# Where ten layers meet: slabs by token tile at each end, token-major openings, and a reordered end of the mixer

## Chip, cores and metric

The kernel runs on one core of one Trainium2 chip. The metric is the device time of one execution in microseconds (us). Beside the runs there is one profiled execution, from which every row below comes.

## What is computed

The reference is a two-block hybrid transformer on 256 tokens of width D = 1024, in float32. Cut to its layers, each with what follows it:

```python
x = LN(a*x + 0.5*swiglu(x))            # phase 0, FFN, 2816 hidden
x = LN(a*x + hybrid_mixer(x))          # phase 1, MIXER
x = LN(a*x + 0.5*swiglu(x))            # phase 2, FFN          a = 2**0.25
h = h + 0.5*swiglu(rms(h))             # phase 3, FFN
h = h + short_conv(rms(h))             # phase 4, CONV: (b * conv(c*u)) @ w_out, b, c, u = split(rms(h) @ w_in)
h = h + 0.5*swiglu(rms(h))             # phase 5, FFN
shared = shared_kv(rms(h))             # phase 6, KV: keys, values, and compressed ones by a GELU MLP
h = h + 0.5*swiglu(rms(h))             # phase 7, FFN
h = h + nsa(rms(h), *shared)           # phase 8, NSA: compressed, selected and window attention, gated
h = h + 0.5*swiglu(rms(h))             # phase 9, FFN
```

The mixer is three attentions of six heads each (MOBA, DIFF, STICK). Each is projected by its branch matrix and weighted by a sigmoid gate, and the sum goes through w_out.

## The kernel before

**Slabs.** All large weights go through one ring of six slots. A slab is 128 x 2048 values (1 MB): half of a 512-wide column block of a projection (kh = 0 or 1, four chunks of 128 rows), or two rows of 128 x 1024 of a matrix that ends a layer. SyncE loads slab k with two DMAs when slab k - 6 has been used (semaphore slab_used). ScalarE (ACT) writes its high half w_hi, VectorE (DVE) the rest w_lo = raw - w_hi. TensorE (PE) makes each product from three matmuls: low by high, high by low, high by high (function product, L1562 to L1564). The input of a layer, transposed, is split in the same way into xT_hi (ACT, L632) and xT_lo (DVE, L977).

**Order.** Each engine has an instruction list written out by hand; there is no planner. On ACT and DVE the call split(k) stands between the other work, LEAD = 4 slabs ahead of the one in use. The semaphores high_ready and low_ready carry them to the next engine. Phases 0 to 9 take 33, 36, 33, 33, 16, 33, 10, 33, 8 and 33 slabs. Tokens are two tiles of 128 (tt = 0, 1).

**End of a layer.** project_slab adds up a closing projection in four PSUM banks Y[tt][half]. All but the last two slabs are taken with both token tiles. Of the last two, first all products of tile 0 are made, which signals y_ready, and then all of tile 1. Meanwhile DVE handles tile 0 in boundary: add_output (L992), layer_norm (L999 to L1002), a root by GpSimd (POOL, L567), layer_norm_apply (L1010, L1012), and rms_norm (L1017, L1023) for which ACT sums the squares (L643). Behind the last product, next_input transposes tile 0 for the next layer (L1571). GpSimd multiplies x by ALPHA beforehand (L606).

**Beginning of a layer.** by_token lets the first column block (two slabs) run over tile 0, puts in the transposes of tile 1, and then runs over tile 1. FFN, MIXER and NSA begin so. CONV and KV begin with slabs by feature, which need the whole input (feature_slab).

**Mixer.** TILES is the order of the column blocks, STEPS how many slabs TensorE takes before head u. Round u + 1 of slabs stands between heads u - 1 and u. DVE forms the maxima (L1141, L1149) and the weights (L1171 to L1180) of a head, normalizes the pairs of DIFF heads (L1188 to L1203), and multiplies branches by gates (L1122 to L1126). The last round is gate 1, branch 0 and branch 1 of STICK, then z_sb is transposed and w_out begins.

**Shared keys.** Slabs 0 and 1 give the raw tokens of the compression by feature. ACT and DVE spread them into xc_hi (L826) and xc_lo (L1317). Slabs 2 and 3 are slot 0 of keys and values, 4 to 7 the compression, 8 and 9 slot 1. ACT applies the GELU (L850) once DVE has made its bias (L1352) from the transposed hidden rows.

**NSA.** Slabs 0 and 1 give the queries of eight heads, then 48 products give the branch gates, then slabs 2 and 3 give the other queries. DVE sums the squares of the queries (L1386), GpSimd takes the roots (L596), DVE scales (L1396) and copies the transposed queries (L1405).

## Time and profile before

| | us |
|---|---|
| median of 3 runs | 1751.81 |
| lowest and highest | 1748.11 and 1752.46 |
| profiled execution, its own time | 1752.8 |
| its span, first to last instruction | 1751.1 |
| TensorE busy (8310 matmuls) | 1677.5 |
| VectorE, ScalarE, GpSimd busy | 968.9, 743.0, 44.3 |

The mean granted clock of TensorE over the span is 0.975 of 2.4 GHz. In the windows below, PE, DVE, ACT and POOL are the engines' busy time; PEld is the weight load, which overlaps PE. Matmuls are pipelined: one of 512 columns is shown with nearly 0.4 us and the next starts 0.23 behind it, so a wait shows as idle only beyond that overlap.

### The profile page before, as it was taken

How to read it: one execution, taken by the hardware profiler on the slowest of the kernel's cores; microseconds unless marked ns; L12 is line 12 of the kernel's file. 1: busy time of each engine (PE TensorE's matmuls, PEld its weight loads, DVE VectorE, ACT ScalarE, POOL GpSimd, SP SyncE). 2: the span in 40 equal slices, each digit the busy share in tenths (PEclk: the TensorE clock that was granted, in tenths of full speed). 3: DMA queues.
4: the chain of work that ended last, by engine and by line, in shares of the span. 5: the costliest groups of instructions: out<-in, count | busy, mean ns of one | idle time of the engine just before them, and what ended most of it. 6: DMA issues, size and time to landing. Idle time of an engine off the chain costs nothing.

```text
span 1751.1 us, 19663 instructions
## 1 busy us (share of the span) xinstructions
PE 1677.5 (96%) x8310; PEld 1402.8 (80%) x8310; DVE 968.9 (55%) x1016; ACT 743.0 (42%) x907; POOL 44.3 (3%) x56
## 2 busy tenths in 40 slices
PE   7999999898799998999999999989999998999998
PEld 6888797776678886888799888878888887888887
DVE  5555557575565546555357555557655454555552
ACT  4544244555344433444234444436444334544441
POOL 1000100000010000000000000000000010000000
PEclk9999999999899999999989999999999997999999
DMA  8565654433455654565546565457465541045551
GB/s 266 178 207 192 193 186 139 133 96 110 136 172 178 222 192 136 182 199 192 180 133 204 170 191 200 175 159 233 153 189 205 175 155 48 1 140 183 184 190 73
DMA packets 226088, 291.13 MB, mean 166 GB/s; under 512 B 10516, under 2 KB 203728, under 8 KB 225872
## 3 DMA queue, kind: packets, MB, share of 16 engines
q1 hardware_dynamic: 226000, 289.87, 50.3%
q8 instruction: 66, 1.08, 0.3%
q14 instruction: 22, 0.18, 0.0%
HBM read 288.78 MB, written 1.05 MB: 166 GB/s over the span
## 4 chain that ended last, share of the span: by engine, by line
PE 88%; DVE 7%; ACT 2%; issue 2%; DMA 0%; POOL 0%; SPq 0%; DVEq 0%; ACTq 0%
PE bank L1562 27%; PE bank L1564 27%; PE bank L1563 26%; DVE w_lo L971 2%; PE bank L1675 2%; PE bank L1961 1%; PE bank L1986 1%; PE bank L1571 1%; PE bank L1971 1%; ACT w_hi L626 1%; DVE xT_lo L977 1%; DVE x_sb L992 1%; ACT xT_hi L632 0%; DMA raw<-in_ffn_w_up_dram 0%; PE bank L2001 0%
## 5 line engine op out<-in xcount | busy, mean ns | idle before, releaser
L971 DVE TENSOR_TENSOR w_lo<-raw,w_hi 128x2048 fp32r<-128x2048 f32 x268 | 609.6, 2286 | 324.9 <-ACT w_hi L626 323.4
L626 ACT ACTIVATE w_hi<-raw 128x2048 fp32r<-128x2048 f32 x268 | 505.0, 1900 | 153.1 <-DMA raw<-in_ffn_w_down_dram 101.0
L1562 PE MATMUL bank<-w_hi,xT_lo 128*128 128x512 f32 (+1 forms) x1328 | 531.3, 400 | 30.1 <-DVE xT_lo L977 17.3
L1564 PE MATMUL bank<-w_hi,xT_hi 128*128 128x512 f32 (+1 forms) x1328 | 521.5, 393 | 0.0
L1563 PE MATMUL bank<-w_lo,xT_hi 128*128 128x512 f32 (+1 forms) x1328 | 520.9, 392 | 0.0
L1562 PEld LDWEIGHTS bank<-w_hi,xT_lo 128*128 128x128 f32 x1328 | 253.7, 191 | 84.5 <-DVE xT_lo L977 20.1
L1564 PEld LDWEIGHTS bank<-w_hi,xT_hi 128*128 128x128 f32 x1328 | 253.2, 191 | 53.5
L1563 PEld LDWEIGHTS bank<-w_lo,xT_hi 128*128 128x128 f32 x1328 | 253.7, 191 | 49.1
L1562 PE MATMUL bank<-w_hi,hT_lo 128*128 128x512 f32 x528 | 209.1, 396 | 0.0
L1563 PE MATMUL bank<-w_lo,hT_hi 128*128 128x512 f32 x528 | 208.6, 395 | 0.0
L1564 PE MATMUL bank<-w_hi,hT_hi 128*128 128x512 f32 x528 | 208.6, 395 | 0.0
L923 ACT ACTIVATE hT_hi<-bank 128x512 fp32r<-128x512 f32 x66 | 39.5, 598 | 213.3 <-PE bank L1675 213.3
L935 ACT ACTIVATE silu<-bank 128x256 f32<-128x256 f32 x132 | 43.6, 381 | 193.4 <-PE bank L1564 193.4
L1564 PEld LDWEIGHTS bank<-w_hi,hT_hi 128*128 128x128 f32 x528 | 99.3, 188 | 23.7
L1563 PEld LDWEIGHTS bank<-w_lo,hT_hi 128*128 128x128 f32 x528 | 99.4, 188 | 23.4
L1562 PEld LDWEIGHTS bank<-w_hi,hT_lo 128*128 128x128 f32 x528 | 99.3, 188 | 23.4
L1562 PE MATMUL bank<-xT_hi,w_lo 128*128 128x256 f32 x368 | 108.4, 295 | 6.8 <-DVE w_lo L971 4.0
L1563 PE MATMUL bank<-xT_lo,w_hi 128*128 128x256 f32 x368 | 107.5, 292 | 0.0
L1564 PE MATMUL bank<-xT_hi,w_hi 128*128 128x256 f32 x368 | 107.4, 292 | 0.0
L1512 DVE TENSOR_TENSOR hT_lo<-bank,hT_hi 128x512 fp32r<-128x512 f32 x66 | 45.6, 691 | 99.6 <-ACT hT_hi L923 99.5
L1523 DVE TENSOR_TENSOR h<-silu,bank 128x256 f32<-128x256 f32 x132 | 49.6, 417 | 74.9 <-ACT silu L935 74.9
L1562 PEld LDWEIGHTS bank<-xT_hi,w_lo 128*128 128x128 f32 x368 | 74.1, 201 | 8.8 <-issue 5.0
(246 smaller groups left out, 1241.0 us busy)
## 6 DMA issues: line engine op xcount, KB each, us to landing
raw<-in_ffn_w_gate_up_dram SPq DMA_DIRECT2D x176, 512.0 KB, 4.7
raw<-in_ffn_w_down_dram SPq DMA_DIRECT2D x132, 512.0 KB, 4.0
raw<-in_ffn_w_gate_dram SPq DMA_DIRECT2D x44, 512.0 KB, 3.9
raw<-in_ffn_w_up_dram SPq DMA_DIRECT2D x44, 512.0 KB, 5.0
raw<-in_w_in_dram SPq DMA_DIRECT2D x44, 512.0 KB, 4.9
raw<-in_conv_w_in_dram SPq DMA_DIRECT2D x24, 512.0 KB, 4.5
raw<-in_kv_w_dram SPq DMA_DIRECT2D x12, 512.0 KB, 4.4
raw<-in_w_out_dram SPq DMA_DIRECT2D x8, 512.0 KB, 3.6
```

Source lines behind the costliest of these rows:

```text
L626: nc.scalar.activation(w_hi[:, slot, 0:width], raw[:, slot, 0:width], ACT.Copy).then_inc(high_ready, 1)
L923: nc.scalar.activation(hT_hi[:, 2 * j:2 * j + 2, :], bank[4 + j % 2][:].rearrange("p (c m) -> p c m", c=2), ACT.Copy).then_inc(hT_high, 1)
L935: nc.scalar.activation(silu[:, tt, :], bank[2 * (j % 2) + tt][:, 0:256], ACT.Silu).then_inc(silu_ready, 1)
L971: nc.vector.tensor_tensor(w_lo[:, slot, 0:width], raw[:, slot, 0:width], w_hi[:, slot, 0:width].bitcast(F32), ALU.subtract).then_inc(low_r ...
L977: nc.vector.tensor_tensor(xT_lo[:, 4 * q:4 * q + 4, tt * P:(tt + 1) * P], src[:].rearrange("p (k m) -> p k m", k=4), xT_hi[:, 4 * q:4 * q ...
L992: ins = nc.vector.scalar_tensor_tensor(out=part, in0=Y[tt][half][:], scalar=factor, in1=part, op0=ALU.mult, op1=ALU.add)
L1512: nc.vector.tensor_tensor(hT_lo[:, 2 * j:2 * j + 2, :], bank[4 + j % 2][:].rearrange("p (c m) -> p c m", c=2), hT_hi[:, 2 * j:2 * j + 2, : ...
L1523: nc.vector.tensor_tensor(h[:, tt, :], silu[:, tt, :], bank[2 * (j % 2) + tt][:, 256:512], ALU.mult).then_inc(h_ready, 1)
L1562: nc.tensor.matmul(o, x_lo, wh, start=first, stop=False, skip_group_check=shared)
L1563: nc.tensor.matmul(o, x_hi, wl, start=False, stop=False, skip_group_check=shared)
L1564: return nc.tensor.matmul(o, x_hi, wh, start=False, stop=last_one, skip_group_check=shared)
L1675: ins = nc.tensor.transpose(dst[:, c, tt * P:(tt + 1) * P], h[:, tt, c * P:(c + 1) * P], ident[:])
```

## The change

Layers end with tail(n) slabs by token tile: four where LN and RMS follow, else three. Tile 0's transposes for the next layer stand ahead of the last slab of tile 1. Each layer but the first begins with four slabs by token. CONV opens with its b gate by token, copies it (conv_b) and transposes it in sixteen transposes; KV opens with slots 0 and 1, the raw tokens come third, and tile 1 of slot 1 behind them. The compressed products move into the next FFN. In NSA all queries precede the gates. In the mixer the order of blocks and steps changes, splits run MIX_LEAD = 5 ahead, and its end takes gate 1 around branch 0. Splits are counted (split_to) instead of placed one by one. The factor ALPHA goes into add_output, with x and the epsilon scaled to match.

```diff
+TAIL = 3
+MIX_LEAD = 5
+        def tail(n):
+            return TAIL + 1 if has_ln(n) and has_rms(n) else TAIL
-        TILES = [("v of moba, sb",), ("q, k of moba",), ("k of moba, q of diff",), ("q, k of diff",), ("v of diff",),
-                 ("gate", MOBA, 0), ("gate", MOBA, 1), ("branch", MOBA, 0), ("branch", MOBA, 1),
-                 ("q, k of sb",), ("k, v of sb",), ("gate", DIFF, 0), ("gate", DIFF, 1), ("branch", DIFF, 0), ("branch", DIFF, 1),
+        TILES = [("v of moba, sb",), ("v of diff",), ("q, k of moba",), ("k of moba, q of diff",), ("q, k of diff",),
+                 ("gate", MOBA, 0), ("gate", MOBA, 1), ("q, k of sb",), ("branch", MOBA, 0), ("branch", MOBA, 1),
+                 ("k, v of sb",), ("gate", DIFF, 0), ("gate", DIFF, 1), ("branch", DIFF, 0), ("branch", DIFF, 1),
                  ("gate", STICK, 0), ("gate", STICK, 1), ("branch", STICK, 0), ("branch", STICK, 1)]
+        MIX_SLABS += [(16, 0), (17, 0), (16, 1), (18, 0)]
-        STEPS = [6] + [1] * 8 + [2] * 3 + [1] * 4 + [2, 1, 1] + [4]
+        STEPS = [8] + [1] * 8 + [2] + [1] * 6 + [2, 1, 1] + [4]
...
 # ACT
+            def split_to(k):
+                while highs[0] <= k:
+                    split(highs[0])
+                    highs[0] += 1
             def boundary(n):
+                split_to(first_slab[n + 1] + 5 - tail(n))
+                if n < last:
                     for tt in range(NT):
                         norm(n, [tt])
                         evacuate_input(inputs_before(n + 1), TOKENS_FIRST[2 * tt:2 * tt + 2], 2 * tt)
+                        if tt == 0:
+                            split_to(first_slab[n + 1] + 3)
...
 # ACT, mixer's end
+                    gate_half(STICK, 0)
+                    split_to(s0 + 34)
+                    evacuate_input(inputs_before(n) + 1, MERGED_FIRST[0:2])
+                    gate_half(STICK, 1)
+                    split_to(s0 + 35)
+                    evacuate_input(inputs_before(n) + 1, MERGED_FIRST[2:4], 2)
...
 # ACT, KV
+                    for kv in range(2):
+                        split_to(s0 + 10 + 2 * kv)
+                        act.wait_ge(slab_used, s0 + 8 + 2 * kv)
                         nc.scalar.activation(hid_row[:, kv, :], bank[6 + kv][0:CMP_ROWS, 0:CMP_HID], ACT.Copy).then_inc(hid_rows, 1)
+                        if kv == 1:
+                            evacuate_input(inputs_before(n + 1), TOKENS_FIRST[0:2])
                         act.wait_ge(bias_ready, kv + 1)
...
 # DVE
             def boundary(n, factor, y_at):
+                split_to(first_slab[n + 1] + 5 - tail(n))
                 for tt in range(NT):
                     add_output(n, tt, factor, y_at)
                     if has_ln(n):
+                        layer_norm(n, tt, factor)
+                        if tt == 1:
+                            split_to(first_slab[n + 1] + (2 if has_rms(n) else 3))
+                        layer_norm_apply(n, tt)
+                    if tt == 1:
+                        split_to(first_slab[n + 1] + 3)
+                    if has_rms(n):
+                        rms_norm(n, tt)
+                    if n < last:
+                        evacuate_input(inputs_before(n + 1), TOKENS_FIRST[2 * tt:2 * tt + 2], 2 * tt)
...
 # DVE, KV
+                    keys_spread(1)
+                    keys_norm(1)
+                    split_to(s0 + 9)
                     for tt in range(NT):
                         rms_norm(n, tt)
                     for kv in range(2):
-                        split(s0 + 8 + 2 * kv)
-                        split(s0 + 9 + 2 * kv)
+                        split_to(s0 + 10 + 2 * kv)
+                        if kv == 1:
+                            evacuate_input(inputs_before(n + 1), TOKENS_FIRST[0:2])
                         dve.wait_ge(hidT_psum, kv + 1)
...
 # DVE, NSA
                     queries_norm(0)
-                    split(s0 + 5)
-                    split(s0 + 6)
-                    queries_out(0)
+                    split_to(s0 + 5)
                     queries_spread(1)
                     queries_norm(1)
+                    split_to(s0 + 6)
+                    queries_out(0)
...
 # PE, in place of project_slab
+                for tt in range(NT):
+                    for d in range(first, slabs):
+                        if tt == 0:
+                            ready(d)
+                            pe.wait_ge(low_ready, s0 + d + 1)
+                        elif d == slabs - 1 and n < last:
+                            next_input(n + 1, 0)
+                        for c in range(2):
+                            ins = part(d, c, tt)
+                        if tt == 1:
+                            ins.then_inc(slab_used, 1)
+                        elif d == slabs - 1:
+                            ins.then_inc(y_ready, 1)
...
+            def by_token(n, works, second=3):
                 for tt in range(NT):
+                    for i, work in enumerate(works):
+                        if tt == 0 and i == second:
                             next_input(n, 1)
+                        pe.wait_ge(xT_ready, 4 * inputs_before(n) + 2 * tt + min(i, 1) + 1)
+                        work(tt)
...
 # PE, mixer's end
+                    for d in ROUND[-1][:-1]:
                         slab(d)
                     pe.wait_ge(merged, 10)
+                    transpose_input(z_sb, MERGED_FIRST[0:2])
+                    slab(ROUND[-1][-1])
...
 # PE, KV
+                    by_token(n, [pairs(slot, kh) for slot in range(2) for kh in range(2)], 2)
                     for kh in range(2):
+                        ins = feature_slab(s0 + 4 + kh, kh, [bank[4], bank[5]], 4)
+                    ins.then_inc(cmp_in_psum, 1)
+                    keys_values(1, 0, 1).then_inc(slab_used, 1)
+                    keys_values(1, 1, 1).then_inc(slab_used, 3)
```

In by_token, second is 2 where the layer before ends without LN.

## Rows read from the trace of the kernel before

**Rows 1.** The page's part 1: busy us of each engine (share) xinstructions.

```profile
PE 1677.5 (96%) x8310; PEld 1402.8 (80%) x8310; DVE 968.9 (55%) x1016; ACT 743.0 (42%) x907; POOL 44.3 (3%) x56
```

**Rows 2.** Waits of TensorE: us in total, times, longest.

```profile
PE bank L1562 <- DVE xT_lo L977: 20.2, 13, 7.6
PE bank L1562 <- DVE w_lo L971: 14.0, 3, 6.0
```

**Rows 3.** Windows: length, busy us (x), PEclk, DMA share, GB/s.

```profile
320.00:340.00 20.00, 16.01 (x113) 15.20 (x111) 11.23 (x22) 8.12 (x18) 0.00 (x0) 0.83 0.33 106
...
440.00:464.00 24.00, 14.47 (x62) 11.41 (x60) 13.23 (x13) 6.60 (x6) 0.00 (x0) 0.79 0.29 92
478.00:494.00 16.00, 13.07 (x57) 10.19 (x56) 10.62 (x15) 3.68 (x5) 3.23 (x3) 0.89 0.42 132
664.00:692.00 28.00, 21.42 (x88) 16.95 (x87) 16.22 (x24) 6.03 (x9) 3.21 (x4) 0.88 0.34 112
868.00:888.00 20.00, 14.68 (x75) 13.18 (x74) 13.25 (x15) 9.86 (x11) 1.10 (x2) 0.74 0.33 106
...
1160.00:1180.00 20.00, 14.64 (x84) 13.14 (x84) 13.55 (x20) 10.06 (x12) 1.10 (x2) 0.83 0.45 138
1220.00:1232.00 12.00, 11.02 (x67) 9.20 (x66) 9.39 (x24) 6.94 (x14) 2.15 (x2) 1.00 0.36 117
...
1430.00:1444.00 14.00, 14.00 (x69) 12.34 (x69) 9.50 (x9) 6.88 (x7) 3.26 (x2) 0.76 0.34 139
```

**Rows 4.** Timeline of DVE at two boundaries: start, us, instruction [idle].

```profile
668.30 1.29 DVE L992 SCALAR_TENSOR_TENSOR x_sb<-bank,x_sb 128x512 f32<-128x512 f32 x2 [7.12 <-PE bank L1564]
...
673.34 1.28 DVE L1012 SCALAR_TENSOR_TENSOR x_sb<-x_sb,stats,gain 128x1024 f32<-128x1024 f32 x1
...
677.56 1.28 DVE L1023 SCALAR_TENSOR_TENSOR z_sb<-x_sb,stats,gain 128x1024 f32<-128x1024 f32 x1
...
866.79 1.29 DVE L992 SCALAR_TENSOR_TENSOR x_sb<-bank,x_sb 128x512 f32<-128x512 f32 x2 [7.27 <-PE bank L1564]
...
870.11 1.29 DVE L1023 SCALAR_TENSOR_TENSOR z_sb<-x_sb,stats,gain 128x1024 f32<-128x1024 f32 x1 [0.66 <-POOL stats L567]
872.39 1.29 DVE L992 SCALAR_TENSOR_TENSOR x_sb<-bank,x_sb 128x512 f32<-128x512 f32 x2 [0.99 <-PE bank L1564]
```

**Rows 5.** The page's parts 5 and 6: splits and loads of slabs.

```profile
L971 DVE TENSOR_TENSOR w_lo<-raw,w_hi 128x2048 fp32r<-128x2048 f32 x268 | 609.6, 2286 | 324.9 <-ACT w_hi L626 323.4
L626 ACT ACTIVATE w_hi<-raw 128x2048 fp32r<-128x2048 f32 x268 | 505.0, 1900 | 153.1 <-DMA raw<-in_ffn_w_down_dram 101.0
...
raw<-in_ffn_w_gate_up_dram SPq DMA_DIRECT2D x176, 512.0 KB, 4.7
```

**Rows 6.** Timeline of DVE in the rounds of DIFF.

```profile
326.87 1.02 DVE L1141 SCALAR_TENSOR_TENSOR prob<-far,bank 128x384 f32<-128x384 f32 x2 [0.71 <-PE bank L1776]
...
333.20 2.29 DVE L971 TENSOR_TENSOR w_lo<-raw,w_hi 128x2048 fp32r<-128x2048 f32 x1
...
338.08 0.43 DVE L1203 TENSOR_TENSOR oT_lo<-o_norm,oT_hi 128x256 fp32r<-128x256 f32 x1 [0.48 <-ACT oT_hi L732]
```

**Rows 7.** Timeline of ACT and of DVE at the shared keys.

```profile
1185.86 4.91 ACT L826 ACTIVATE xc_hi<-bank 64x512 fp32r<-64x512 f32 x8 [6.15 <-PE bank L1564]
...
1212.69 0.52 ACT L850 ACTIVATE hid<-bank,cmp_bias 128x64 f32<-128x64 f32 x2 [5.58 <-DVE cmp_bias L1352]
...
1188.34 5.72 DVE L1317 TENSOR_TENSOR xc_lo<-bank,xc_hi 64x512 fp32r<-64x512 f32 x8 [3.94 <-ACT xc_hi L826]
...
1201.14 0.76 DVE L1335 TENSOR_TENSOR key_n<-bank,key_ms 128x256 f32<-128x256 f32 x2 [1.76 <-POOL key_ms L600]
...
1206.83 1.28 DVE L1023 SCALAR_TENSOR_TENSOR z_sb<-x_sb,stats,gain 128x1024 f32<-128x1024 f32 x1 [0.66 <-POOL stats L567]
```

**Rows 8.** Timeline of POOL and of DVE at the queries of NSA.

```profile
1451.95 3.24 POOL L596 TENSOR_TENSOR q_ms<-q_ms,minus_half 128x8 f32<-128x8 f32 x2 [14.17 <-DVE q_ms L1387]
...
1449.13 1.41 DVE L1405 TENSOR_SCALAR qT<-bank,cols 128x512 f32<-128x512 f32 x2 [6.16 <-PE bank L1925]
```

More of the change, by code:

```diff
@@ L47 @@
 PHASES = [FFN, MIXER, FFN, FFN, CONV, FFN, KV, FFN, NSA, FFN]
-BY_TOKEN = (FFN, MIXER, NSA)
+CONV_AT = PHASES.index(CONV)
 LENGTH = {FFN: 33, MIXER: 36, CONV: 16, KV: 10, NSA: 8}
@@ L811, in _ @@
-                    for d in range(KC // 2 - 2):
-                        split(s0 + 12 + d + LEAD)
+                    split_to(s0 + 4)
+                    for half in range(2):
+                        act.wait_ge(slab_used, s0 + 2 * half + 2)
+                        for tt in range(NT):
+                            nc.scalar.activation(conv_b[:, tt, 512 * half:512 * (half + 1)], bank[2 * half + tt][:], ACT.Copy)\
+                                .then_inc(conv_b_ready, 1)
+                        split_to(s0 + 5 + 2 * half)
@@ L1209, in tiles @@
                                 tile_out(ends(d))
-                    def slabs(steps):
-                        for d in steps:
-                            split(s0 + d + LEAD)
                     for d in ROUND[0]:
@@ L1250, in _ @@
+                    tile_out(TILES.index(("branch", STICK, 0)))
+                    split_to(s0 + 34)
+                    tile_out(TILES.index(("gate", STICK, 1)))
+                    evacuate_input(inputs_before(n) + 1, MERGED_FIRST[0:2])
+                    tile_out(TILES.index(("branch", STICK, 1)))
+                    split_to(s0 + 35)
+                    evacuate_input(inputs_before(n) + 1, MERGED_FIRST[2:4], 2)
                     boundary(n, 1.0, s0 + 36)
-                    for d in range(KC // 2 - 2, KC // 2):
-                        split(s0 + 32 + d + LEAD)
@@ L1681, in tile, with first_tiles, work @@
                         gate_up(j, 1)
-                    by_token(n, lambda kh, tt: gate_up(0, kh, tiles=[tt]))
+                    def first_tiles(j, kh):
+                        def work(tt):
+                            if behind_kv(n) and (j, kh, tt) == (1, 0, 0):
+                                pe.wait_ge(key_normed, 2)
+                            gate_up(j, kh, [tt])
+                            if behind_kv(n) and (j, kh, tt) == (0, 0, 0):
+                                transpose_hidden(1)
+                            if behind_kv(n) and (j, kh, tt) == (0, 0, 1):
+                                compressed()
+                            if (j, kh, tt) == (1, 0, 1):
+                                hidden(0)
+                        return work
+                    if n == 0:
+                        by_token(n, [first_tiles(0, kh) for kh in range(2)])
+                        tile(1)
+                    else:
+                        by_token(n, [first_tiles(j, kh) for j in range(2) for kh in range(2)], 2 if not has_ln(n - 1) else 3)
                     def transpose_keys(slot, b):
```

537 lines of the change are left out of this document (232 added, 305 removed).

## The prediction, made before the change was run

> **What bounds the kernel now.** I read the page first: TensorE is busy 1677.5 us of a span of 1751.1, so it sets the time, and only what leaves it idle or slow can be won [rows 1]. The waits of TensorE say whom it waits for: for the low halves of the layer's input, 20.2 us in 13 waits, the longest 7.6; for low halves of weights, 14.0 us in three, of which 6.0 is the first load, so that two are 4.0 [rows 2]. The windows then show where, and what each stretch loses beside the idle time: the reader is to see PE busy below the length, and PEclk below 1.00 in the same stretch [rows 3]. PEclk 0.83 over 20 us means 6.8 us at 1.2 instead of 2.4 GHz; what TensorE does in them takes twice as long. So the mixer's first wait costs 4.0 idle and some 3.1 of slow clock; there are two of them. The mixer's end loses 9.5 idle and 2.3 clock; the boundary FFN to FFN 6.6 and 3.1; FFN to convolution 5.3 and 3.2; FFN to shared keys 5.4 and 2.5. Boundaries without LN where the next layer already opens by token lose 1.0 to 1.1 and no clock (1220:1232; those at 974, 1415 and 1557 are alike).
>
> The other engines are loose in the mean (DVE 55%), but they run in order, and what matters below is what stands ahead of the needed instruction. Unit costs: twelve products of one token tile and one slab take 2.8 us (the two adds of one boundary start 5.60 apart, with 24 products between) [rows 4]. A slab that comes free is split 9.4 us later: landing 4.7, high half 1.9, low half 2.3, and 0.5 for issuing [rows 5]. From the first add to the normalized tile DVE needs 6.3 us with LN, 10.5 with LN and RMS, 4.6 with RMS alone [rows 4]; without the two operations for the other tile that stand inside the 10.5, it is 9.7.
>
> **Projections end with three or four slabs by token, layers open with four (all nine boundaries).** Call T the start of the last three slabs. The first token tile is ready at T+8.4 (before: two slabs, 5.6), the second takes as long, and the transposes for the next layer now stand before its last slab, so 5.6 us of products cover the norm and the last 2.8 cover the 2.6 that ACT and DVE need to split the transposed tile. The price is a slab less of lead: before the first add DVE must split the next layer's third slab, whose slot is free only at T, so the add starts at T+9.4.
> - RMS alone (five: 872, 974, 1165, 1415, 1557 us): normalized at T+14.0, TensorE there at T+14.0: no wait. Second tile: add 1.3, a split 2.3, spread, root and scaling 2.1 make 5.7 against two slabs of the new layer, 5.6: 0.2 wait. At the convolution this leaves 0.3 of 5.3 and no slow clock: -8.2 with the 3.2; with the second tile's transposes now under products, another 1.0: -9.2. At the shared keys 5.4+2.5 go the same way: -7.9. The three that lost 1.1 give 0.8 each: -2.4, of which NSA's is counted below, so -1.6.
> - LN alone, FFN to mixer: normalized at T+9.4+6.3=T+15.7, 1.7 late; second tile 0.4 and 0.5, because a slab of v of diff is narrower. Before, 2.8 in three waits. 0.
> - LN alone, mixer to FFN: the three waits of 1.0 and half of 3.4 us of clock (478:494) [rows 3] become one wait of 1.9: -2.7.
> - LN and RMS, FFN to FFN, four slabs: no late split (11.2 before the first add). The tile comes 9.7 after the add, cover is 8.4: 1.3. Second tile: add and statistics 3.0, split 2.3, LN 2.6, split 2.3, RMS 2.1 = 12.3 against three slabs, 8.2: a wait of 4.1 where before it was 1.0, and slow clock again, 2.5. 5.4+2.5 for 6.6+3.1: -1.8.
> - The scaling of x by ALPHA on GpSimd goes into the add's scalar, an operation of the same form; it ran beside splits for which TensorE did not wait: 0. Were that cover gone, three splits a little slower would be at stake, some 3 us in all.
>
> **Mixer.** v of diff moves to the front, q, k of sb two rounds earlier, splits run five slabs ahead instead of four. The two low halves that were late are then split three rounds sooner. Their 8.0 idle and 6.2 clock go. But the three double rounds of DIFF become one. DVE needs 6.3 us from a head's scores to its weights with a split in it (326.87 to 333.20) and in every second round 3.1 more for the pair's norm (to 338.51), plus 0.7 for the copy of v of sb [rows 6]; TensorE has 5.8 of a slab, 0.9 of outputs and 0.3 of transposes for it. So 10.1 stand against 6.8: one wait of 3.2 at the twelfth head, 0.5 in small ones, and 2.5 of clock: 14.2 become 6.2, -8.0. The bounds are none of it (-12, the splits being earlier still) and a wait in every second of the rounds. At the end, the gate's second half is computed between the branches, so that transposes, sigmoids and half of the sums lie under 4.1 us of branch and 5.6 of first projection slab. DVE has nothing left behind the last branch but 2.7 for 5.6 of products. All of the idle time there goes, 9.5, and 2.3 of clock: -11.8. A wait would take its place only if banks 6 and 7, into which the first transposes now go, were read late; attention has left them a slab before.
>
> **Convolution.** Four slabs of 5.8 become token slabs of 5.5 (-1.2), 16 transposes of 0.11 are added (+1.8): +0.6. DVE has 10.6 us of work for each 11.5 of products.
>
> **Shared keys.** Time from the layer's first product. Two halves of slot 1 now wait until after the feature slabs, which end at 29.1. Then 5.6 of token products and 6.8 + 6.8 of compression; before, 11.4 and the last key slabs of 11.4 lay around them. DVE in order: the eight low halves of xc start 2.5 behind ACT's copies, as at 1188.34 after 1185.86, and last 5.7: 37.3 [rows 7]; norm of the keys, 3.4 with 1.8 of waiting for GpSimd's roots: 40.7; two splits: 45.3 (the first needed at 41.4: 1.6 late); two RMS tiles, 0.1+0.7+1.3 each, 4.1: 49.4; a split and the bias: 51.9. ACT waits for this bias before its GELU, as it does now for 5.6 us [rows 7], and only behind it stand its splits of the next two slabs (56.2), the row copy (56.6) and the copy of the transposed input (57.7). DVE's splits end at 58.9, its first input half at 59.6. TensorE is through with keys and transposes at 51.2: it waits 8.4. The fourth slab of the FFN is split behind the second input tile, 2.2 late. 12.2 for today's 1.0 (1220:1232) [rows 3]: +11.2, and about 4 of slow clock that is not there now: +15.2.
>
> **NSA.** Both query slabs now precede the branch gates. The chain for queries of the second half (5.5 us, of which GpSimd's roots are 3.2 [rows 8]) and two splits now stand on DVE ahead of the copy of the first transposed queries. From the first product: first low split 19.0 (its slab is issued behind the gate weights), queries 24.5, split 26.8, queries 32.3, split 34.6, copy 1.4: 36.0 [rows 8]. TensorE is through with transposes at 29.8: waits 6.2. Today it needs 35.6 us from the end of the projection to its first scores; then 36.9: +1.3. Today's 6.8 us at the lower clock fall on the gate products (1430:1444, 14.00 busy of 14 at 0.76) [rows 3] and on dense ones behind them; then they are longer and fall on the scores: +2.5. Together +3.8.
> The Trainium skill, TensorE: Matmul & The Clock Gate, Part 4 (PE-mode transpose), says that transposes do not count as activity as products do; by it the transposes behind the gates would prolong the slow stretch, and this would be +3.4 instead of +2.5, the sum -22.5. The trace has no such sequence without a wait in it, so I keep 2.5.
>
> **Sum.** 0 -2.7 -1.8 -9.2 -7.9 -1.6 -8.0 -11.8 +0.6 +15.2 +3.8 = -23.4. The profiled execution took 1752.8 (span 1751.1), the median of the runs is 1751.8: forecast 1728.4, say 1728.
>
> **Rivals.**
> 1. The new waits at the shared keys and NSA do not come, because slabs land sooner or ACT is ahead. For it: DVE is busy only 55% in the mean; against: the bias stands behind norms and splits in DVE's order, and ACT stands still for it already now [rows 7]. Then -19: 1709.
> 2. DVE becomes the bound in DIFF and STICK rounds of the mixer. For it: the 10.1 against 6.8 above; against: DVE was busy 11.2 of 20 at 320 [rows 3]. If more rounds than one wait 3 to 4, four in all, the mixer's middle gives +2 instead of -8: 1738.
> 3. Slower: a slab's lead is lost at nine boundaries. If the third slab's split comes later than the 9.4 us that I take, the add and all behind it are late. Were it behind two other splits on DVE, 4.6 us [rows 5], that would be eight times 4.6 = 37, less 23: 1766. It decides from 2.9 us a boundary. Against it: in the down phase DVE sits idle 7 us before the add [rows 4].
> 4. No effect: what is won at boundaries is given back at the keys, NSA and in the mixer by more slow clock than taken: 1750.
>
> **How the numbers follow.** Forecast 0.6, rival 1 0.12, rival 2 0.16, rival 4 0.06, rival 3 0.06. The measurement tells 0.3% (5 us). The forecast's own bounds: waits at the keys 8 to 16, mixer's middle -12 to -4, clock at either level in 5 stretches +-5: 1716 to 1739. To hold 8 in 10 it reaches toward rivals 1 and 2: 1711 to 1743. Faster 0.90, same 0.05, slower 0.05.
>
> **What would show it.** Right: adds that start a little over one microsecond behind the third slab's end, no slow stretch at 872 and 1165, none in the mixer's middle but one, the first w_out slab 20 us behind the last head, a wait of 8 us before FFN 7 on xT_lo, one of 6 before the first NSA scores, one of 4 inside the first slabs after 674. Wrong: the add's idle time ended by ACT w_hi late by several microseconds; waits for w_lo in the FFNs.

## The result, and the profile after it

The changed kernel takes 1733.7 us (median of 6 runs, 1729.97 to 1743.8) against 1751.65 of the kernel before on the same chip: a ratio of 0.990, 95% interval 0.988 to 0.992, or 18 us less. The forecast was 1728 with a range of 1711 to 1743, so the median lies in it, 6 us on the slow side; five of the six executions took 1730 to 1734 and one 1743.8. The profiled execution took 1733.36 (span 1731.6); the row of each engine answers to [rows 1]:

```profile
PE 1673.9 (97%) x8230; PEld 1391.2 (80%) x8230; DVE 966.8 (56%) x1016; ACT 746.4 (43%) x910; POOL 32.5 (2%) x53
```

TensorE is busy 3.6 us less in a span that is 19.5 shorter: what went is idle time. Its waits, against [rows 2]:

```profile
PE bank L1530 <- DVE w_lo L977: 9.3, 3, 5.6
PE bank L1539 <- DVE z_sb L1039: 7.8, 10, 4.2
PE bank L1530 <- DVE xT_lo L991: 7.4, 1, 7.4
...
PE bank L1984 <- DVE qT L1379: 3.7, 1, 3.7
PE bank L1539 <- DVE x_sb L1030: 3.2, 4, 1.9
PE bank L1841 <- ACT o_norm L761: 2.8, 1, 2.8
```

The rows of DVE at the boundary to the shared keys, start, us, instruction, idle before; they answer to [rows 4]:

```profile
1121.62 2.29 DVE L977 TENSOR_TENSOR w_lo<-raw,w_hi 128x2048 fp32r<-128x2048 f32 x1 [3.27 <-ACT w_hi L635]
1123.83 1.28 DVE L1010 SCALAR_TENSOR_TENSOR x_sb<-bank,x_sb 128x512 f32<-128x512 f32 x2
```

The add now stands behind a late split and is no longer waiting for PE. Of the waits, thirteen for the low half of the input (xT_lo) have become one, of 7.4 us, and those of the transposes for the normalized rows (z_sb) went from 12.9 us in three to 7.8 in ten. The one for the transposed queries (qT) grew from 1.1 to 3.7, and one of 2.8 in the mixer (o_norm) is new. The windows of the same places as in [rows 3], in their order: the DIFF rounds, the mixer's end, mixer to FFN, FFN to FFN, FFN to convolution, FFN to shared keys, shared keys to FFN 7 (two), and NSA's gates and first scores. The columns are again length, busy us of PE, PEld, DVE, ACT and POOL, PEclk, DMA share, GB/s.

```profile
342.00:362.00 20.00, 17.09 (x63) 12.16 (x63) 14.05 (x30) 10.81 (x24) 0.00 (x0) 0.74 0.17 56
428.00:452.00 24.00, 24.00 (x115) 19.98 (x114) 18.48 (x18) 11.52 (x11) 0.00 (x0) 1.00 0.54 171
452.00:468.00 16.00, 14.11 (x67) 11.51 (x66) 12.42 (x18) 2.89 (x3) 2.60 (x2) 1.00 0.63 198
644.00:672.00 28.00, 22.49 (x98) 17.84 (x97) 19.33 (x21) 9.99 (x11) 3.62 (x3) 0.94 0.45 148
840.00:860.00 20.00, 19.53 (x93) 15.66 (x93) 12.31 (x15) 8.19 (x10) 1.10 (x2) 1.00 0.48 158
1124.00:1144.00 20.00, 19.85 (x95) 15.95 (x94) 12.92 (x21) 9.55 (x12) 1.10 (x2) 1.00 0.48 157
1172.00:1192.00 20.00, 10.86 (x73) 10.21 (x73) 15.88 (x15) 12.69 (x15) 1.47 (x3) 0.91 0.96 309
1200.00:1208.00 8.00, 5.80 (x21) 4.35 (x20) 3.58 (x3) 2.50 (x3) 0.00 (x0) 0.84 0.00 0
1416.00:1452.00 36.00, 30.04 (x121) 24.93 (x120) 18.02 (x31) 12.58 (x40) 3.23 (x2) 0.53 0.07 22
```

The reader is to see three things. At the mixer's end PE is busy 24.00 of 24 at 1.00, where it was 14.47 of 24 at 0.79. Where an FFN meets the convolution or the keys, it is busy 19.5 to 19.9 of 20 at 1.00 instead of 14.7 at 0.74 and 0.83. And the last row is new: 36 us at 0.53, nearly all of it at 1.2 GHz.

To set this against the forecast, the execution is cut into stages, each from one boundary's add for the second token tile (L1010 or L1007) to the next one's. For each stage the trace gives its length, TensorE's idle time, and the busy time in stretches at 1.2 GHz, of which half counts as lost. Differences after minus before, in us:

| Stage | Length before | after | Difference | Idle | Clock | Forecast: idle | clock |
|---|---|---|---|---|---|---|---|
| FFN 0 | 204.3 | 204.3 | 0.0 | 0.0 | +2.1 | 0 | 0 |
| mixer | 277.1 | 258.5 | -18.6 | -14.5 | -3.7 | -13.8 | -6.0 |
| FFN 2 | 193.2 | 190.4 | -2.8 | -1.2 | -1.7 | -1.0 | -1.7 |
| FFN 3 | 197.8 | 195.2 | -2.6 | -1.4 | -1.2 | -1.2 | -0.6 |
| convolution | 102.2 | 95.0 | -7.2 | -4.1 | -4.1 | -5.4 | -3.2 |
| FFN 5 | 189.9 | 189.0 | -0.9 | -1.0 | 0.0 | -0.8 | 0 |
| keys, FFN 7 | 250.6 | 257.8 | +7.2 | +5.2 | +0.9 | +5.8 | +1.5 |
| NSA | 142.2 | 149.1 | +6.9 | +2.0 | +5.0 | +1.3 | +2.5 |
| FFN 9 | 189.4 | 187.9 | -1.5 | -0.9 | 0.0 | -0.8 | 0 |
| sum | 1751.1 | 1731.6 | -19.5 | -15.9 | -2.8 | -15.9 | -7.5 |

Both sums take in the last 4.3 us of the span; what idle and clock leave of a difference is the products themselves and the transposes. The idle time came as forecast in sum; its parts are off by up to 1.3 us either way (convolution -4.1 for -5.4, mixer -14.5 for -13.8, keys +5.2 for +5.8, NSA +2.0 for +1.3), so that the sums agree to 0.1 is luck. The clock gave back 2.8 us where 7.5 were forecast. NSA is the largest part of that gap.

### The profile page after: what moved, and what is told of

Its sections match the earlier page's. It is cut to its first block, busy times and chain, and to the rows that moved or that the text cites. A ratio compares the mean times of both kernels' runs of the same rounds, so it can differ in the third digit from the quotient of the medians.

```text
span 1731.6 us, 19555 instructions
## 1 busy us (share of the span) xinstructions
PE 1673.9 (97%) x8230; PEld 1391.2 (80%) x8230; DVE 966.8 (56%) x1016; ACT 746.4 (43%) x910; POOL 32.5 (2%) x53
## 4 chain that ended last, share of the span: by engine, by line
PE 82%; DVE 9%; ACT 3%; issue 2%; DMA 2%; POOL 1%; SPq 0%; DVEq 0%; POOLq 0%; ACTq 0%
PE bank L1530 24%; PE bank L1532 24%; PE bank L1531 24%; DVE w_lo L977 3%; PE bank L1989 2%; PE bank L1691 2%; ACT w_hi L635 1%; PE bank L1539 1%; PE bank L2014 1%; POOL stats L580 1%; DVE z_sb L1039 1%; PE bank L1999 1%; DVE x_sb L1010 1%; DMA raw<-in_w_in_dram 1%; DVE bn L1017 0%
## 5 line engine op out<-in xcount | busy, mean ns | idle before, releaser
L977 DVE TENSOR_TENSOR w_lo<-raw,w_hi 128x2048 fp32r<-128x2048 f32 (+1 forms) x268 | 608.0, 2275 | 345.4 <-ACT w_hi L635 344.3
L635 ACT ACTIVATE w_hi<-raw 128x2048 fp32r<-128x2048 f32 (+1 forms) x268 | 507.6, 1901 | 204.8 <-DMA raw<-in_ffn_w_down_dram 100.8
L1530 PE MATMUL bank<-w_hi,xT_lo 128*128 128x512 f32 (+1 forms) x1360 | 540.9, 398 | 18.0 <-DVE w_lo L977 7.8
L1532 PE MATMUL bank<-w_hi,xT_hi 128*128 128x512 f32 (+1 forms) x1360 | 531.8, 391 | 0.0
L1531 PE MATMUL bank<-w_lo,xT_hi 128*128 128x512 f32 (+1 forms) x1360 | 530.7, 390 | 0.0
L1531 PEld LDWEIGHTS bank<-w_lo,xT_hi 128*128 128x128 f32 x1360 | 258.4, 190 | 50.4
L1530 PE MATMUL bank<-xT_hi,w_lo 128*128 128x256 f32 x304 | 86.8, 286 | 0.0
L1531 PE MATMUL bank<-xT_lo,w_hi 128*128 128x256 f32 x304 | 86.0, 283 | 0.0
L1532 PE MATMUL bank<-xT_hi,w_hi 128*128 128x256 f32 x304 | 86.0, 283 | 0.0
L649 ACT ACTIVATE xT_hi<-bank 128x512 fp32r<-128x512 f32 x48 | 26.3, 595 | 104.6 <-PE bank L1539 104.6
```

The lines of the kernel that those rows point to most:

```text
L635: nc.scalar.activation(w_hi[:, slot, 0:width], raw[:, slot, 0:width], ACT.Copy).then_inc(high_ready, 1)
L649: nc.scalar.activation(xT_hi[:, 4 * q:4 * q + 4, tt * P:(tt + 1) * P], src[:].rearrange("p (k m) -> p k m", k=4), ACT.Copy).then_inc(xT_hi ...
L977: nc.vector.tensor_tensor(w_lo[:, slot, 0:width], raw[:, slot, 0:width], w_hi[:, slot, 0:width].bitcast(F32), ALU.subtract).then_inc(low_r ...
L1530: nc.tensor.matmul(o, x_lo, wh, start=first, stop=False, skip_group_check=shared)
L1531: nc.tensor.matmul(o, x_hi, wl, start=False, stop=False, skip_group_check=shared)
L1532: return nc.tensor.matmul(o, x_hi, wh, start=False, stop=last_one, skip_group_check=shared)
```

## The experiments

Twelve runs follow: the changed kernel once more, and eleven kernels that start from it or from a better one made of it. Ratios are to the kernel before, on the same chip. First four single steps.

**Queries copied before the split.**

```diff
                     queries_norm(1)
-                    split_to(s0 + 6)
                     queries_out(0)
+                    split_to(s0 + 6)
```

> Only NSA's order on DVE changes: the copy of the first transposed queries stands ahead of the split of the eleventh slab instead of behind it. Theory A (the clock): the gates' products, each 48 columns wide, bring the clock down, and what follows them in the changed kernel (transposes, the wait, scores) does not bring it up again; so the wait before the first scores falls from 3.7 to about 1.5 us (second half's norm ends at 1422.1, the copy takes 1.4, TensorE is there at 1422.0), the long stretch at 1.2 GHz stays, and the stage goes from 149.1 to about 147: -2, some 1731.5. Rival B (the wait itself holds the clock down): with most of the wait gone the scores run at 2.4 GHz, another 5 us go, the stage comes to 142: -7, some 1727.

Measured: 1734.13 us, ratio 0.990 (0.989 to 0.992): nothing won. The first row below is its wait, the second its windows row of the same place.

```profile
PE bank L1984 <- DVE qT L1379: 1.7, 1, 1.7
```

```profile
1416.00:1461.00 45.00, 40.60 (x155) 33.49 (x155) 22.35 (x40) 13.98 (x43) 3.24 (x2) 0.51 0.04 12
```

The wait went from 3.7 to 1.7, and the stretch at 1.2 GHz from 34.1 to 44.4 us; the stage stayed at 149.0. So rival B fell: with 2 us of the wait gone the clock stayed down all the same. Theory A had the long stretch right and its gain of 2 us wrong, since the stretch grew by what the wait gave back. A shorter wait alone is worth nothing here.

**Gates between the queries.** The two last query slabs of the second token tile now stand behind the gates' 48 products (branch_gates_in):

```diff
-                    by_token(n, [lambda tt, j=j, kh=kh: project_queries(j, kh, [tt]) for j in range(2) for kh in range(2)], 2)
...
+                    def queries_in(j, kh):
+                        def work(tt):
+                            if (j, kh, tt) == (1, 0, 1):
+                                branch_gates_in()
+                            project_queries(j, kh, [tt])
+                        return work
+                    by_token(n, [queries_in(j, kh) for j in range(2) for kh in range(2)], 2)
```

ACT takes the gates' sigmoid ahead of the second half's squares, and DVE the copy of the first queries ahead of the second half's sums.

> The branch gates' products are put ahead of the last two query slabs of the second token tile, so that 5.6 us of products of 512 columns stand between them and the transposes; ACT and DVE take up the first half's squares, gates and copies in the order of the kernel before. Theory A: the clock is back at 2.4 GHz before the scores, and there is no wait before them: the stage falls from 149.1 to the 142.2 of the kernel before or a little under (141 to 142): -7 to -8, some 1726. Rival B (only the wait of 3.7 was lost, the slow clock belongs to transposes and scores whatever stands ahead): -3.7, the stage at 145.4, some 1730. Rival C: one waits for the new order elsewhere (the second half's queries come late): no gain.

Measured: 1731.56 us, ratio 0.988 (0.986 to 0.990); the stage is 142.6 in its profile. The windows are the gates, the scores and what follows:

```profile
1411.00:1419.00 8.00, 8.00 (x37) 7.38 (x37) 2.75 (x7) 2.37 (x3) 3.26 (x2) 0.57 0.26 104
1419.00:1435.00 16.00, 12.65 (x72) 9.77 (x70) 10.38 (x15) 6.42 (x8) 3.23 (x2) 1.00 0.42 132
1435.00:1457.00 22.00, 19.59 (x88) 17.74 (x89) 13.80 (x28) 10.06 (x37) 0.00 (x0) 0.61 0.00 1
```

The clock falls under the gates as before, and the first scores run at 2.4 GHz again, as theory A had it, behind a wait of 1.1: -6.6 in the stage. The median moved by 2 only, which the intervals of the two don't tell from nothing. The profile is of the second shortest of six executions (1727.9; they took 1726.0 to 1734.5), and a single profile of NSA is a weak witness.

**First input ahead of the biases.** On ACT, with the row copy and the GELUs left out (DVE likewise):

```diff
                     for kv in range(2):
-                        split_to(s0 + 10 + 2 * kv)
+                        split_to(s0 + 10 + kv)
                         act.wait_ge(slab_used, s0 + 8 + 2 * kv)
...
-                        if kv == 1:
-                            evacuate_input(inputs_before(n + 1), TOKENS_FIRST[0:2])
+                    evacuate_input(inputs_before(n + 1), TOKENS_FIRST[0:2])
+                    for kv in range(2):
+                        split_to(s0 + 12 + kv)
                         act.wait_ge(bias_ready, kv + 1)
...
```

> Only the end of the shared keys is reordered on ACT and DVE: the first token tile of FFN 7's input is copied and split ahead of the biases and GELUs and right behind the split of the twelfth slab; the splits of the thirteenth and fourteenth slab go between the biases, ahead of the second token tile. Theory A (order, as in the forecast's working): the wait for the first tile's low half falls from 7.4 us to about 2 (1.1 for ACT's copy, 1.3 for DVE's), the 2.2 us wait for the fourteenth slab goes, and the slow clock behind them (10.2 us at 1.2 GHz, 5.1 lost) with them; the stage goes from 257.8 to 245 to 248: -10 to -13, some 1722. Rival (DVE has more work there than TensorE has cover, 9.3 of 12 us busy): the wait moves to a later slab or the second tile, and only 3 us are won, some 1731.

In the changed kernel DVE and then ACT do this ahead of the first product of FFN 7, which starts at 1191.5; TensorE has been there since 1184.0. Start, duration, instruction:

```profile
1183.71 0.22 DVE L1331 TENSOR_TENSOR cmp_bias<-bank,cols 128x1 f32<-128x1 f32 x2
1186.31 4.49 DVE L977 TENSOR_TENSOR w_lo<-raw,w_hi 128x2048 fp32r<-128x2048 f32 x2 [2.38 <-ACT w_hi L635]
1190.72 1.28 DVE L991 TENSOR_TENSOR xT_lo<-bank,xT_hi 128x512 fp32r<-128x512 f32 x2
```

```profile
1183.96 0.52 ACT L863 ACTIVATE hid<-bank,cmp_bias 128x64 f32<-128x64 f32 x2 [3.38 <-DVE cmp_bias L1331]
1184.37 3.71 ACT L635 ACTIVATE w_hi<-raw 128x2048 fp32r<-128x2048 f32 x2
...
1188.23 1.07 ACT L649 ACTIVATE xT_hi<-bank 128x512 fp32r<-128x512 f32 x2
```

ACT stands 3.38 us for the bias and does two splits and a row copy before it comes to the input. With the new order:

```profile
1181.36 4.49 DVE L977 TENSOR_TENSOR w_lo<-raw,w_hi 128x2048 fp32r<-128x2048 f32 x2
1185.76 1.28 DVE L991 TENSOR_TENSOR xT_lo<-bank,xT_hi 128x512 fp32r<-128x512 f32 x2
1186.96 0.21 DVE L1330 TENSOR_TENSOR cmp_bias<-bank,cols 128x1 f32<-128x1 f32 x2
```

Measured: 1728.39 us, ratio 0.987 (0.985 to 0.989). The wait is 2.5 instead of 7.4, the 2.2 of the fourth slab is gone, and no slow stretch follows: the stage goes from 257.8 to 247.5, inside the 10 to 13 of theory A. The time fell by 5 only. Its profile, of the longest of its four executions (1732.2), shows why that one was long: NSA had 61.5 us at 1.2 GHz, in stretches of 44.4 and 17.1, and took 158.5 in all.

**Two slabs by token instead of three.**

```diff
-TAIL = 3
+TAIL = 2
```

> TAIL = 2 for 3: projections end with two slabs by token tile (three at FFN to FFN), and the order around them follows. Theory A (cover, the forecast's working): DVE still splits the new layer's next slab ahead of the add, 9.4 us after its slot is free, the normalized tile comes 14 us after the start of the last two slabs, TensorE is there at 11.2: a wait of 2.8 with about 2.5 of slow clock at each of the five boundaries with RMS alone, 2.8 more at each of those with LN: +25 to +38, 1760 to 1771. Rival (the forecast's third, lead): a slab less by token gives back a slab of lead and the add comes sooner: no loss, or a gain of some us.

Measured: 1791.1 us, ratio 1.023 (1.021 to 1.026), 57 us slower than the changed kernel. DVE at the boundary to the shared keys; the add's predecessor is the split that it must wait for:

```profile
1161.03 2.29 DVE L977 TENSOR_TENSOR w_lo<-raw,w_hi 128x2048 fp32r<-128x2048 f32 x1 [3.67 <-ACT w_hi L635]
1163.24 1.28 DVE L1010 SCALAR_TENSOR_TENSOR x_sb<-bank,x_sb 128x512 f32<-128x512 f32 x2
...
1166.55 1.28 DVE L1039 SCALAR_TENSOR_TENSOR z_sb<-x_sb,stats,gain 128x1024 f32<-128x1024 f32 x1 [0.66 <-POOL stats L580]
```

```profile
PE bank L1539 <- DVE z_sb L1039: 37.1, 7, 6.1
PE bank L1539 <- DVE x_sb L1030: 13.7, 2, 8.0
```

The waits at the RMS boundaries are 5.6 to 6.1, not the 2.8 expected. The mechanism was right, its arithmetic was not: TensorE comes to the transposes with the last slab of the second tile still to do, so two slabs cover 8.4 us and not 11.2, and 14.2 (add at 9.7, normalized 4.5 later) less 8.4 is the 5.8 seen. The add stands 9.7 us behind the slab's start, as in the changed kernel (9.5): taking a slab less by token brought no earlier add, so the run's rival (lead) fell, and the cover decides. A split that comes later than the 9.4 us, as in the forecast's third rival, is not in this run. Its profile is of the longest of four executions (1799.6; the others took 1789.5 to 1791.7): against the changed kernel it has 40 us more idle time and 28 us more lost to the clock, of which 8.5 is a stretch of 17.1 us at 1.2 GHz in NSA.

**The changed kernel again, and the steps together.** The spread of NSA asks for a second look at the same kernel.

> The changed kernel itself, taken once more, since two kernels with the same products in NSA showed slow stretches of 34 and 44 us there. Theory A (the length of the slow stretch in NSA is not set by the program alone): NSA's stage differs from the 149.1 of the first profile by some us in either direction, while every other stage agrees within 1.5 us; the six times spread over 8 us or more again (1730 to 1744 before). Rival (it is set by the program): the same 34 us at the same place, the stage at 149 within 0.5.

Measured: 1733.93 us (1731.49 to 1742.24), ratio 0.991 (0.989 to 0.994). Its profile has the same 34.1 us stretch at the same place, and a stage of 149.1: the rival was right for the profile. The six times were 1731.5 to 1734.3 four times and 1742.1 and 1742.2. A second level 8 us up is what a further stretch of 17.1 us would cost, and such a stretch stands some 110 to 120 us into the stage in four other kernels' profiles (one at 1494 below). That the slower executions here had one is likely: their mean granted clock is 0.971 against 0.977 to 0.979 in the other four, and 17.1 us at half the clock are 0.005 of it. No profile of them was taken. Nor is the length of the long stretch set by NSA's own code alone: of the seven profiles in which that code is the same, six have 34.1 us, and the one of the keys above has 44.4.

> The two reorders together: FFN 7's first input tile ahead of the biases at the end of the shared keys, and the branch gates ahead of the last two query slabs of the second token tile. If they add up by the medians of their runs (1728.4 and 1731.6 against 1733.7): 1726. By the stages of their profiles (-10.3 and -6.6): 1717. The stage of keys and FFN 7 at 247.5, NSA at 143. Rival (the slow stretch in NSA comes back whatever stands ahead of it, as it did in the keys run): NSA at 150 to 158, 1728 to 1732.

Measured: 1716.98 us (1716.29 to 1718.13), ratio 0.980 (0.979 to 0.982): 36 us under the kernel before, 17 under the changed one, the best median of all here and what the stages said (247.5 and 143.7 in its profile). A stretch of 20.5 us at 1.2 GHz still stands behind the first scores, at 1425. The wait ahead of it, and the windows of gates, scores and what follows:

```profile
PE bank L2037 <- DVE qT L1378: 3.1, 1, 3.1
```

```profile
1401.00:1408.00 7.00, 7.00 (x29) 6.32 (x29) 2.62 (x5) 2.05 (x2) 2.94 (x2) 0.54 0.20 72
1408.00:1425.00 17.00, 12.78 (x72) 9.88 (x71) 11.00 (x17) 7.37 (x14) 3.23 (x2) 0.99 0.37 124
1425.00:1446.00 21.00, 19.46 (x82) 17.16 (x83) 11.89 (x23) 8.03 (x31) 0.00 (x0) 0.51 0.00 1
```

**Gates mixed in among wide products.** In this one each chunk's six narrow products (beside) stand ahead of three wide ones:

```diff
                 for c in range(4):
+                    if beside:
+                        beside(c)
                     for tt in tiles:
```

> As the run of both reorders, but the 48 narrow products of the gates (48 columns each) are not in a row: they stand in threes between the wide products of two query slabs of the second token tile (six narrow behind every three wide). Theory A (many narrow products in a row are what takes the clock down): no slow stretch before the scores, NSA's stage 2 to 5 us under that of both reorders, 138 to 141, and less spread between the times. Rival (the scores, transposes and waits take it down on their own): a slow stretch begins at the scores all the same, no more than 1 us between the two kernels.

Measured: 1718.36 us (1711.73 to 1727.28), ratio 0.981 (0.979 to 0.984).

```profile
1384.00:1426.00 42.00, 37.32 (x208) 30.86 (x207) 23.88 (x32) 17.17 (x25) 9.05 (x12) 1.00 0.51 168
1426.00:1447.00 21.00, 19.45 (x82) 17.16 (x83) 11.92 (x23) 8.06 (x31) 0.00 (x0) 0.51 0.00 1
1494.00:1512.00 18.00, 18.00 (x78) 16.88 (x77) 5.12 (x9) 2.28 (x4) 0.00 (x0) 0.53 0.00 1
```

The stretch at the gates is gone (42 us at 1.00), as theory A had it, but in the profile, of the longest execution, a stretch of 17.1 us came at 1494. It makes the stage 149.0; less the 8.5 that it costs, that is 140.5, inside theory A's 138 to 141. The times stand on two levels: the three shortest (1711.7 to 1714.3, granted clock 0.987 to 0.991) lie under all of the run before it, the three longest (1722.5 to 1727.3, all at 0.981) over. So the median is the same, and the spread grew instead of shrinking.

**Few gates.** The rival cause, tested by a kernel that leaves out seven eighths of the gates' products, so that they come from an eighth of the input.

```diff
-                        for c in range(KC):
+                        for c in range(1):
```

> The run of both reorders with seven eighths of the branch gates' products left out: 6 narrow products of the first chunk stay of 48 (the gates are then computed from an eighth of the input). Theory A (narrow products in a row start the first slow stretch, the scores and transposes the second on their own): the 6.8 us stretch at 1401 is gone, the one of 17 to 20 us at the scores stays; NSA's stage falls by the products' 5.3 us and 1 to 3 of clock, 143.7 to 135.5 to 137.5. Rival (the second stretch is the first one's after-effect): the scores run at 2.4 GHz, 8 to 10 us more, the stage at 127 to 129.

Measured: 1719.08 us, ratio 0.980 (0.976 to 0.984). The first row is the wait ahead of the scores, then the windows:

```profile
PE bank L1992 <- DVE qT L1378: 2.4, 1, 2.4
```

```profile
1381.00:1408.00 27.00, 23.97 (x116) 19.40 (x114) 14.61 (x18) 13.01 (x15) 5.81 (x10) 1.00 0.75 249
1408.00:1446.00 38.00, 35.39 (x131) 28.87 (x132) 20.78 (x38) 11.65 (x40) 3.24 (x2) 0.51 0.03 9
```

The first stretch is gone, as theory A had it; for the second both fell. With 42 of 48 narrow products left out, some 5 us, the stage is 0.4 shorter (143.3), since the clock falls in the wait ahead of the scores (at 1408.1) and 37.5 us pass before that ends. Narrow gates are one way into a long stretch and not the only one; here a wait of 0.7, transposes and a wait of 2.4 stand ahead of the scores.

**Late split.** DVE splits one w_o slab behind the first maxima of the scores, to take the 3.1 us wait above away.

> The run of both reorders with one more step: DVE splits the eleventh... the third of the projection's slabs behind the maxima of the first two score units, not ahead of them. In that run's trace the copy of the second transposed queries comes 3.15 us late, since the split and the first maxima stand ahead of it. Theory A: the maxima then lie under the second scores, the copy follows the transposes at once, the wait falls to about 1.5, and the exponentials come 2 us sooner: -2 to -3, 1714 to 1715. Rival (the slow stretch that begins at the scores grows by what is won): 1717 within 1.

Measured: 1723.0 us (1722.04 to 1727.21), ratio 0.984 (0.981 to 0.986), 6 us worse than both reorders (0.979 to 0.982, on another chip).

```profile
PE bank L1991 <- ACT sel_pT L902: 3.3, 1, 3.3
...
PE bank L2036 <- DVE qT L1378: 1.1, 1, 1.1
```

The wait went from 3.1 to 1.1, and the one for the transposed weights behind it from 1.5 to 3.3: ACT's exponentials then bound these units, and the step won 0.4 us of idle time. What made the stage 5.4 longer (149.0) is the clock, 5.9 by the same count as in the table: the profile has another 17.1 us stretch, at 1490.

**Three single steps of the mixer and the adds.** The transposes of the mixer's end behind the last branch slab, the lead back at four, and the scaling back on GpSimd:

```diff
+                    slab(ROUND[-1][-1])
                     pe.wait_ge(merged, 10)
                     transpose_input(z_sb, MERGED_FIRST[0:2])
-                    slab(ROUND[-1][-1])
```

```diff
-        MIX_LEAD = 5
+        MIX_LEAD = 4
```

> One step of the mixer's end is undone: TensorE transposes the first half of the merged heads behind the last branch slab instead of ahead of it (as in the kernel before); DVE and ACT keep their order. By the forecast's working the branch slab (4.1 us) is the cover of 1.1 for ACT's copy and 1.3 for DVE's, so a wait of 2.4 to 3.0 comes ahead of the first slab of w_out, with 0 to 3 of slow clock: +3 to +6, some 1738. Rival (cover isn't what the new end gives; the sums and the gate's place are): nothing is lost, 1734 within 1.

Measured: 1736.84 us, ratio 0.992 (0.990 to 0.994), which the intervals don't tell from the changed kernel's on that chip (0.989 to 0.994). The profile does show the step: the stage is 3.0 longer, with this new wait ahead of the first slab of w_out, 1.6 and not the 2.4 to 3.0 expected. Another 1.7 comes from 3.4 us at 1.2 GHz at the boundary 22 us later, which the changed kernel's profile doesn't have; whether the new wait causes it is not shown.

```profile
PE bank L1530 <- DVE xT_lo L991: 1.6, 1, 1.6
```

> Only MIX_LEAD goes back from 5 to 4: in the mixer each slab is split one slab later than in the changed kernel; the new order of the tiles and of the rounds stays. Theory A (the rounds' order took the two waits of 4.0 away, the lead only helps): 0 to 3 us lost, 1734 to 1737. Rival (the lead did it): low halves of weights are late again in rounds that take a slab each, two waits of about 4 us with their slow clock, 8 to 14 us lost, 1742 to 1748.

Measured: 1735.44 us, ratio 0.991 (0.988 to 0.994); the mixer's stage is 257.6 against 258.5, and no low half of a weight is late in it. So the new order of column blocks and rounds did it, which no run takes apart; the fifth slab of lead wins nothing that can be seen.

> Only the scaling of the residual by ALPHA goes back to GpSimd, one operation over both token tiles in each of the three layers with LN, with the add's scalar at 1. The forecast put its removal at 0, since it ran beside splits for which TensorE does not wait: 1734 within 1. Rival (the shared access slows splits that now have less cover): up to 3 us slower.

Measured: 1735.15 us, ratio 0.990 (0.987 to 0.993): nothing clear of the noise, as forecast. GpSimd's operation took 5.38 us, and all the 260 splits of full width took 596.6 us on DVE against 594.0 without it, 2.6 us over the three layers that TensorE never waited for.

## Why the prediction was right, and where it was off

- **Boundaries.** Right at seven of nine. In the changed kernel the add to the keys starts at 1123.83, 9.5 us behind the third-last slab's start (forecast 9.4); at four of the five RMS boundaries TensorE waits 0.3 us at most, and no slow stretch follows; the waits of mixer to FFN and FFN to FFN are 1.9, 1.3 and 4.2 for 1.9, 1.3 and 4.1. Two are off: FFN to mixer waits 0.8 where 1.7 was forecast, and convolution to FFN 1.0 where none was, since DVE and ACT come to the late split from the convolution's own work and the add starts 10.3 behind the slab's start. The two-slab run shows that it is the cover that does it.
- **Convolution.** -7.2 for -8.6: it kept 1.2 us of idle time instead of 0.3, 1.0 of it the wait at its end, and what idle and clock leave of the stage came out 1.0 longer than before; more slow clock went than forecast (4.1 for 3.2).
- **Mixer.** -18.6 for -19.8. From the end of the last head to the add 56.6 became 46.1 us, -10.5 for -11.8; the rest gave -8.1 for -8.0, with one wait of 2.8 at the place where 3.2 was forecast (TensorE's three parts there, 5.8, 0.9 and 0.3, make 7.0 and not the 6.8 that it used, hence 3.1). That the splits' lead had a share in it is not seen: the run with a lead of four loses nothing.
- **Shared keys.** Right: waits of 1.5, 7.4 and 2.2 for 1.6, 8.4 and 2.2, the stage +7.2 for +7.3. The first input stood behind the bias, the GELU and two splits, and with it ahead of them 10.3 us came back. The waits came, so the first rival (no such waits) is out, and they were a matter of order.
- **NSA.** This is the step that failed, as the size of one term: "then they are longer and fall on the scores: +2.5". The stage gave +6.9 for +3.8. DVE's chain was right within 0.3 us in each of its steps: from the first product at 1390.0 the first queries are normalized at +24.4 (24.5), the second at +32.1 (32.3), and the first copy ends at +35.7 (36.0). TensorE got there 2.2 us later than forecast, since its gates' products took 1.3 longer and its eight transposes 0.9, both at 1.2 GHz, and so it waited 3.7 instead of 6.2. It begins the scores 35.5 us behind the add of the boundary, as before the change, where the forecast had 36.9: the 2.0 more of idle time up to there is offset by as much less of busy time, and the whole +6.9 comes behind that point. These rows answer to [rows 8]:

```profile
1418.12 3.23 POOL L609 TENSOR_TENSOR q_ms<-q_ms,minus_half 128x8 f32<-128x8 f32 x2 [4.41 <-DVE q_ms L1361]
```

```profile
1421.38 0.76 DVE L1370 TENSOR_TENSOR sel_pT<-bank,q_ms 128x256 f32<-128x256 f32 x2 [0.84 <-POOL q_ms L609]
1422.06 2.28 DVE L977 TENSOR_TENSOR w_lo<-raw,w_hi 128x2048 fp32r<-128x2048 f32 x1
1424.26 1.41 DVE L1379 TENSOR_SCALAR qT<-bank,cols 128x512 f32<-128x512 f32 x2
```

 There the clock, down since the gates' products (1417.0), did not come back for 34.1 us in all. The groups of instructions (instruction, shape, count | busy us, mean ns | idle) show the first unit's 16 score products, first in the changed kernel and then in the run of both reorders:

```profile
L1989 PE MATMUL bank<-k_sel,qT 64*128 64x128 f32 (+1 forms) x16 | 5.5, 534 | 0.0
```

```profile
L1997 PE MATMUL bank<-k_sel,qT 64*128 64x128 f32 (+1 forms) x16 | 2.9, 331 | 0.0
```

 Slow stretches in NSA are 40.9 us in all, 27.3 before, which is +5.0 in busy time where 2.5 were taken. The trace of before has the first scores at 2.4 GHz, with two wide slabs between them and the gates; with 24 wide products, 5.6 us, put back between (gates between the queries) they are at 2.4 again. I priced the gates' stretch and took its end for granted.

The Trainium skill, TensorE: Matmul & The Clock Gate, Part 4 (PE-mode transpose), says that transposes don't count as activity as products do. The forecast gave that rule +3.4; the clock cost +5.0, nearer to the rule than to my 2.5. Of the runs, behind wide products, transposes and a wait of 1.1 the scores start at 2.4 GHz, and behind the same with a wait of 0.7 ahead of the transposes and one of 2.4 behind them (few gates) at 1.2. That agrees with the rule taken together with the wait; it doesn't single the rule out.

- **The rest of the clock.** The slow stretches gave 2.8 back instead of 7.5. Besides NSA, 2.3 of this is in the mixer (its wait of 2.8 is followed by 10.2 us at 1.2 GHz, one of 2.7 at 394.9 by 6.8, where the forecast had one slow stretch in the mixer's middle) and 2.1 is a stretch of 6.8 us at 11 us, in FFN 0, where the kernels do the same work; of 13 profiles since the change 6 have it.
- **Left open.** What decides how long a stretch in NSA lasts, and what starts the one of 17.1 us deep in its attention, which stands in the profiles of four kernels (keys, two slabs, gates mixed, late split). Those of 34.1 and 44.4 us start under the gates' products, that of 37.5 in the wait ahead of the scores, those of 20.5 behind it; none of the runs controls it. Nor does a run take the openings by token apart from the ends by token, or the order of the column blocks from that of the rounds.

## What to carry to other kernels

A boundary between layers is a sum of cover and chain: count what TensorE still has to do from the signal to its own wait, including where the transposes stand in it, and the wait follows, here within half a microsecond at seven of nine boundaries and within one at the other two; a slab less of cover at each cost 57 us, waits and slow clock together. Where one engine serves two purposes, put what TensorE waits for next ahead of what it will need later: one such swap at the keys took 10 us off its stage, and made with the one in NSA it nearly doubled the gain of the whole change. And price a wait together with what follows it: ahead of light work the clock, once down, stayed down for 34 us, and with the wait cut by 2 us for 44, so that the cut gave nothing. Where a time stands on two levels, as here, a single profile or a difference of medians under 9 us has to be read with the granted clock of each execution.

## What was not expected of the hardware

- TensorE at 1.2 GHz for 34 to 44 us on end while it was busy 30.0 of 36 us, and 40.6 of 45: the work in it is the last of the gates' products, transposes, score products of 32 to 256 columns and outputs, and it did not bring the clock up. Ahead of wide products the stretches are 3.4 to 10.2 us long.
- Under 48 products of 48 columns in a row the clock fell with PE busy 8.00 of 8 us (0.57 in that window, gates between the queries); with three wide products behind each six, or with six alone, there was no such stretch.
- The same program gives times on two levels 8 us apart (four of 1731.5 to 1734.3, two of 1742, with a mean granted clock of 0.977 to 0.979 and 0.971). The Trainium skill, TensorE: Matmul & The Clock Gate, Part 1, says that the monitor behind the clock runs free of the kernel, so that equal programs see it at different phases. The stretch at 11 us that comes and goes in equal work agrees with that.
